# A two-block model in fp32r parts on one core: MLP bias rows in parts, softmax scaling moved to ScalarE, attention heads begun inside projections, and turns of the identity ahead of five waits

## The reference

```
def first_block(x, c, positions, ...):
    for i in range(2):
        shift, scale, gate = modulation(silu(c), mod_mix_w[i], mod_mix_b[i])
        h = x * (1.0 + scale) + shift
        y = mla_mixer(h, ...) if i == 0 else s5_mixer(h, ...)
        x = layer_norm(ALPHA * x + (1.0 + gate) * y, ...)
        shift, scale, gate = modulation(silu(c), mod_ffn_w[i], mod_ffn_b[i])
        a = relu((x * (1.0 + scale) + shift) @ w1 + b1)
        x = layer_norm(ALPHA * x + (1.0 + gate) * ((a * a) @ w2 + b2), ...)
    return x

def second_block(x, ...):
    for l in range(2):
        x = macaron_ffn(x, ...)             # x + 0.5 * rms_norm(swiglu(rms_norm(x)))
        xn = rms_norm(x)
        if l == 0: m = recurrent_block(xn)  # RG-LRU, ends in (h * gelu(y)) @ w_out + b_out
        else:      m = moba_attention(xn @ w_q, k, v, rel_bias) @ w_o
        x = x + rms_norm(m)
        x = macaron_ffn(x, ...)
        if l == 0: k, v = shared_kv(x)
    return x
```

## Time and profile before

| | |
|---|---|
| median of 3 runs | 1750.84 us (1749.12 to 1753.19) |
| profiled execution | 1750.2 us |
| its span, first to last instruction | 1748.6 us |
| mean granted TensorE clock | 0.969 of full |
| PE busy | 1646.2 us (94%) |
| DVE, ACT, POOL busy | 1147.3, 839.1, 153.8 us |

### The profile page before, as it was taken

How to read it: one execution, slowest core, us unless ns; L and a number is a source line. 1 busy time by engine, 2 the same in 40 slices (tenths; PEclk the granted TensorE clock), 3 DMA queues, 4 the chain that set the end, 5 groups by cost and what they waited for, 6 DMA issues and landing times.

```text
span 1748.6 us, 20517 instructions
## 1 busy us (share of the span) xinstructions
PE 1646.2 (94%) x8221; PEld 1327.7 (76%) x8221; DVE 1147.3 (66%) x1354; ACT 839.1 (48%) x1134; POOL 153.8 (9%) x293
## 2 busy tenths in 40 slices
PE   7778999988988999999999999999999999799998
PEld 3656787875677788878888868888788888578887
DVE  4699778888969665575546876544754546665554
ACT  3553465544234555544335875334634435553433
POOL 4510100026600100000000000000000000000000
PEclk9878999999999999999999989999999999899999
DMA  9838588752036566445654554555555554245551
GB/s 305 310 126 308 185 302 332 288 214 100 1 142 220 193 227 238 161 168 192 225 184 141 199 189 171 192 192 169 207 178 183 186 188 167 96 144 193 193 191 74
DMA packets 145096, 335.45 MB, mean 192 GB/s; under 512 B 18213, under 2 KB 34061, under 8 KB 143850
## 3 DMA queue, kind: packets, MB, share of 16 engines
q1 hardware_dynamic: 134310, 293.65, 48.8%
q0 software_dynamic: 9696, 37.29, 5.6%
q10 hardware_dynamic: 996, 3.20, 0.5%
HBM read 328.86 MB, written 6.83 MB: 192 GB/s over the span
## 4 chain that ended last, share of the span: by engine, by line
PE 71%; DVE 16%; ACT 5%; issue 4%; POOL 2%; DMA 1%; SPq 1%; DVEq 0%; ACTq 0%; POOLq 0%
PE ps L670 22%; PE ps L672 22%; PE ps L671 22%; DVE wlo L1794 3%; PE ps L755 2%; ACT whi L1253 1%; DMA operands<-in_mod_mix_w 1%; PE ps L749 1%; DVE work L2247 1%; DVE xlo L1799 1%; PE ps L762 1%; DVE B L1927 1%; POOL mod L2509 1%; DVE B L1926 1%; DVE small L1859 1%
## 5 line engine op out<-in xcount | busy, mean ns | idle before, releaser
L1794 DVE TENSOR_TENSOR wlo<-raw,whi 128x2048 fp32r<-128x2048 f32 (+2 forms) x247 | 559.8, 2283 | 253.5 <-ACT whi L1253 252.2
L1253 ACT ACTIVATE whi<-raw 128x2048 fp32r<-128x2048 f32 (+2 forms) x247 | 466.9, 1908 | 233.9 <-PE ps L672 170.5
L670 PE MATMUL ps<-whi,xhi 128*128 128x512 f32 (+2 forms) x1244 | 477.5, 384 | 18.9 <-DVE xlo L1799 17.3
L672 PE MATMUL ps<-whi,xlo 128*128 128x512 f32 (+2 forms) x1244 | 471.8, 379 | 0.0
L671 PE MATMUL ps<-wlo,xhi 128*128 128x512 f32 (+2 forms) x1244 | 471.7, 379 | 0.0
L670 PE MATMUL ps<-whi,hhi 128*128 128x512 f32 x736 | 294.6, 400 | 6.2 <-DVE hlo L1799 5.2
L671 PE MATMUL ps<-wlo,hhi 128*128 128x512 f32 x736 | 289.0, 393 | 0.0
L672 PE MATMUL ps<-whi,hlo 128*128 128x512 f32 x736 | 288.8, 392 | 0.0
L670 PEld LDWEIGHTS ps<-whi,xhi 128*128 128x128 f32 x1244 | 235.5, 189 | 64.6 <-DVE xlo L1799 21.0
L672 PEld LDWEIGHTS ps<-whi,xlo 128*128 128x128 f32 x1244 | 235.5, 189 | 44.2
L671 PEld LDWEIGHTS ps<-wlo,xhi 128*128 128x128 f32 x1244 | 235.8, 190 | 41.7
(11 more groups left out here) (371 smaller groups left out, 1599.8 us busy)
## 6 DMA issues: line engine op xcount, KB each, us to landing
raw<-in_mlp_w SPq DMA_DIRECT2D x64, 1024.0 KB, 5.6
raw<-in_ffn_w_gate SPq DMA_DIRECT2D x44, 1024.0 KB, 5.1
raw<-in_ffn_w_up SPq DMA_DIRECT2D x44, 1024.0 KB, 5.2
raw<-in_ffn_w_down SPq DMA_DIRECT2D x44, 1024.0 KB, 4.9
mod<-in_mod_ffn_w POOLq DMA_DIRECT2D x16, 1024.0 KB, 6.9
mod<-in_mod_mix_w POOLq DMA_DIRECT2D x12, 1024.0 KB, 7.4
operands<-in_mod_mix_w SPq DMA_DIRECT2D x8, 1024.0 KB, 8.5
raw<-in_lru_w_in SPq DMA_DIRECT2D x8, 1024.0 KB, 5.2
```

Source lines behind the costliest of these rows:

```text
L670: pe.matmul(o, lh, rh, start=start, stop=False)
L672: return pe.matmul(o, ll, rh, start=False, stop=stop)
L1253: act.activation(whi[:, c % SPL, 0:n], raw[:, c % RAW, 0:n], ACT.Copy).then_inc(hi_done, 1)
L1794: dve.tensor_tensor(wlo[:, c % RAW, 0:n], raw[:, c % RAW, 0:n], whi[:, c % SPL, 0:n].bitcast(F32), ALU.subtract).then_inc(lo_done, 1)
```

## The change

Six edits, in one diff.

- **Bias rows of the MLPs.** `open_acc` is gone from `mlp`. Instead `down(..., biased=name)` of the first hidden slice issues, for each bank, two one-row fp32r matmuls ahead of the first product, after the waits for `brow_lo_ok` and `hid_ok`. The row's high part is an ACT copy of 1x1024 (and, for `mlp0`, a copy of the ones), between `hi(c+4)` and `hi(c+5)`. Its rest is a DVE operation of 1x1024 between `lo(c+4)` and `lo(c+5)`.
- **Turns of the identity.** `keep_busy(bank, n)` turns the identity `n` times into a free bank: 14 in `turn(name, 1)` of `mlp0`, `s5` and `ffn10`, 28 in `mla` ahead of `zn_ok`, 32 in `s5` ahead of `g_ok`.
- **First attention.** The rotary queries of heads 0 to 3 are turned before the second half's rotary projection, and `attention` begins after `q_ok` 2 and `qt_ok` 1; the other turns and waits stand in `beside_attention`. ACT's `hi(5)` stands between its two copies of the rotary queries.
- **Softmax scaling.** In both attentions DVE only takes the reciprocal, into `recips`; ACT scales the probabilities of head `i-1` by two copies after the exponentials of head `i`.
- **Second attention.** The scores of heads 0 and 1 stand between the projections of tiles 0 and 1 of the second slice, those of head 2 after tile 1, ahead of the turns. ACT's copies and `hi(c+5)`, `hi(c+6)` are interleaved; DVE's `lo(c+6)` moves into step 0.
- **LRU.** `open_acc("lru")`, with its wait `lg_ok`, stands ahead of `turned(3)`.

```diff
@@ down
+                        if biased and k == 0:
+                            half = slice(512 * n, 512 * (n + 1))
+                            pe.matmul(ps[:, 2 * tt + n, :], ones_r[0:1, :], brow_hi[:, half], start=True, stop=False)
+                            last = pe.matmul(ps[:, 2 * tt + n, :], ones_r[0:1, :], brow_lo[biased][:, half], start=False, stop=False)
+                            if tt and n:
+                                last.then_inc(acc_open, 1)
+            def keep_busy(bank, n):
+
+                for _ in range(n):
+                    pe.transpose(ps[:, bank, 0:P], ident[:, :], ident[:, :])
@@ turn
+                if tt and name in ("mlp0", "s5", "ffn10"):
+                    keep_busy(x_bank(1, 0), 14)
@@ mlp on PE
-                    if i == 0:
-                        open_acc(name)
                     for tt in range(T):
+                        if i == 0:
+                            acc_ready(name, tt)
+                            pe.wait_ge(brow_lo_ok, MLPS.index(name) + 1)
                         pe.wait_ge(hid_ok, HID0[name] + 2 * i + tt + 1)
-                        down(mlp_down(name, i, 0), 4 * (i % 2), tt)
+                        down(mlp_down(name, i, 0), 4 * (i % 2), tt, biased=name if i == 0 else None)
@@ mla on PE
+                keep_busy(0, 28)
                 for tt in range(T):
                     pe.wait_ge(zn_ok, tt + 1)
...
+                    if g:
+                        turn_rotary(0)
...
-                pe.wait_ge(q_ok, 4)
-                pe.wait_ge(qt_ok, 2)
+                pe.wait_ge(q_ok, 2)
+                pe.wait_ge(qt_ok, 1)
                 attention(0, qT, kT, V, True)
@@ s5 on PE
+                keep_busy(6, 32)
                 pe.wait_ge(g_ok, 2)
@@ lru on PE
-                turned(3)
                 pe.wait_ge(lg_ok, KT)
                 open_acc("lru")
+                turned(3)
                 pe.wait_ge(hg_lo, 1)
@@ mlp on ACT
                 hi(c + 4)
+                if l == 0:
+                    act.activation(ones_r[:, :], ones[0:1, :], ACT.Copy)
+                act.wait_ge(brow_in, 16 * (l + 1))
+                act.activation(brow_hi[:, :], brow[name], ACT.Copy).then_inc(brow_hi_ok, 1)
                 hi(c + 5)
@@ attention on ACT
+                    if 1 <= i <= HEADS:
+                        s = (i - 1) % 3
+                        act.wait_ge(rc_ok, HEADS * n + i)
+                        for tt, (lo, up) in enumerate(((0, P), (P, 3 * P))):
+                            last = act.activation(sms[:, s, lo:up], sms[:, s, lo:up], ACT.Copy, scale=recips[:, 2 * s + tt:2 * s + tt + 1])
+                        last.then_inc(p_ok, 1)
@@ mlp on DVE
                     lo(c + j)
+                    if j == 4:
+                        dve.wait_ge(brow_hi_ok, MLPS.index(name) + 1)
+                        rest(brow_lo[name][:, :], brow[name], brow_hi[:, :]).then_inc(brow_lo_ok, 1)
@@ attention on DVE
-                        do(dve.reciprocal(newton[:, 0:2], atts[:, 2 * s:2 * s + 2]))
-                        dve.tensor_scalar(sms[:, s, 0:P], sms[:, s, 0:P], newton[:, 0:1], None, ALU.mult)
-                        dve.tensor_scalar(sms[:, s, P:3 * P], sms[:, s, P:3 * P], newton[:, 1:2], None, ALU.mult).then_inc(p_ok, 1)
-                        dve.wait_ge(p_ok, e + 1)
+                        dve.reciprocal(recips[:, 2 * s:2 * s + 2], atts[:, 2 * s:2 * s + 2]).then_inc(rc_ok, 1)
```

More of the change, by code:

```diff
@@ L708, in project_narrow, with down @@
                 last.then_inc(pe_pass, 1)
-            def down(c, tile, tt, first=False, final=False, src=(hhi, hlo)):
+            def down(c, tile, tt, first=False, final=False, src=(hhi, hlo), biased=None):
                 chunk_ready(c)
@@ L965, in mla, with turn_rotary @@
                 spread_third(1, (6, 7))
+            def turn_rotary(g):
+                pe.wait_ge(qp_ok, g + 1)
+                for r in range(2):
+                    for tt in range(T):
+                        last = pe.transpose(ps[:, 4 * g + 3, r * L + tt * P:r * L + (tt + 1) * P], qp_tok[:, g, tt, r * P:(r + 1) * P], ident[:, :])
+                last.then_inc(qt_ps, 1)
             def z_pass(c, tt):
@@ L997, in beside_attention @@
             def beside_attention(i):
+                if i == 0:
+                    turn_rotary(1)
                 if i == 1:
+                    pe.wait_ge(q_ok, 4)
+                    pe.wait_ge(qt_ok, 2)
                     same_step()
@@ L1020, in beside_attention, with scores, attention @@
                     spread_third(0, (6, 7))
-            def attention(n, q, k, v, rotary):
+            def scores(n, i, q, k, rotary):
+                h, e = i, HEADS * n + i
+                if i >= 3:
+                    pe.wait_ge(sm_ok, e - 2)
+                for lo, hi, tt, keys in ((0, P, 0, P), (P, 3 * P, 1, L)):
+                    last = pe.matmul(ps[:, h % 3, lo:hi], q[:, h, tt * P:(tt + 1) * P], k[:, h, 0:keys], start=True, stop=not rotary)
+                    if rotary:
+                        a = 64 * (h % 2)
+                        last = pe.matmul(ps[:, h % 3, lo:hi], qpT[a:a + 64, h // 2, tt * P:(tt + 1) * P], kpT[a:a + 64, 0:keys],
+                                         start=False, stop=True)
+                last.then_inc(s_ps, 1)
+            def attention(n, q, k, v, rotary, scored=0):
                 sms, pts = (sm, sm2)[n], (pt, pt2)[n]
                 for i in range(HEADS + 3):
[L1026 to L1030, removed]
-                            last = pe.matmul(ps[:, h % 3, lo:hi], q[:, h, tt * P:(tt + 1) * P], k[:, h, 0:keys], start=True, stop=not rotary)
-                            if rotary:
-                                a = 64 * (h % 2)
-                                last = pe.matmul(ps[:, h % 3, lo:hi], qpT[a:a + 64, h // 2, tt * P:(tt + 1) * P], kpT[a:a + 64, 0:keys],
-                                                 start=False, stop=True)
-                        last.then_inc(s_ps, 1)
+                    if scored <= i < HEADS:
+                        if n and i == 4:
+                            pe.wait_ge(feat_ok, FEAT0["att"] + 4)
+                        scores(n, i, q, k, rotary)
                     if 2 <= i < HEADS + 2:
@@ L1185, in att @@
                     token_turn("att", 0, tt)
-                for tt in range(T):
-                    project("att", c + 3, slice_bank(1, tt), tt, 1)
+                project("att", c + 3, slice_bank(1, 0), 0, 1)
+                acc_ready("att", 1)
+                pe.wait_ge(feat_ok, FEAT0["att"] + 2)
+                scores(1, 0, qT2, kT2, False)
+                scores(1, 1, qT2, kT2, False)
+                project("att", c + 3, slice_bank(1, 1), 1, 1)
+                scores(1, 2, qT2, kT2, False)
                 for tt in range(T):
                     token_turn("att", 1, tt)
-                acc_ready("att", 1)
-                pe.wait_ge(feat_ok, FEAT0["att"] + 4)
-                attention(1, qT2, kT2, V2, False)
+                attention(1, qT2, kT2, V2, False, scored=3)
                 for tt in range(T):
@@ L1506, in mla @@
                     act.activation(qpT[:, 2 * g:2 * g + 2, :].rearrange("p r l -> p (r l)"), ps[:, 4 * g + 3, :], ACT.Copy).then_inc(qt_ok, 1)
[L1507 removed]
+                    if g == 0:
+                        hi(5)
                 attention(0)
@@ L1716, in att @@
                 hi(c + 4)
-                hi(c + 5)
                 for tt in range(T):
                     feature_copy("att", 0, tt, qT2)
-                for tt in range(T):
-                    token_copy("att", 1, tt, c + 3, x_scale("ffn11", tt))
+                hi(c + 5)
+                token_copy("att", 1, 0, c + 3, x_scale("ffn11", 0))
                 hi(c + 6)
+                token_copy("att", 1, 1, c + 3, x_scale("ffn11", 1))
                 for tt in range(T):
@@ L2187, in attention @@
                         piece(6)
+                    if n and i == 0:
+                        lo(FIRST["att"] + 6)
             def s5():
@@ L2361, in att @@
                 c = FIRST["att"]
-                for j in range(3, 7):
+                for j in range(3, 6):
                     lo(c + j)
```

19 lines of the change are left out of this document (11 added, 8 removed).

## The result

The changed kernel takes 1768.61 us in the median (1767.83 to 1769.27, 4 runs), the kernel before 1751.30 (1749.12 to 1753.19): a ratio of 1.0102, 95% interval 1.0087 to 1.0117. It is slower, as forecast, but by 17.3 us (medians) where 9.5 was forecast, and outside the range. The profiled execution has a span of 1767.3 us, 18.7 more than before, at the same mean clock of 0.969.

What follows compares the result with a forecast made beforehand. PE was taken to bound the kernel (71% of the chain, busy 94% of the span). The terms summed to +10.25 us, taken as +9.5 on 1750.2, giving 1759.7; range 1750 to 1765.5.

Steps and rivals of the forecast that it cites:

- MLP bias rows, +6.0: Both MLPs at `hid_ok`: DVE's rest 1.2 us plus eight exposed rows 1.8, +3.0 each; bounds +1.9 to +9.6 for both.
- eight one-row matmuls of 512 columns: Behind each MLP's wait for `hid_ok`: priced from three products at 0.227 us each, 1.8 in all.
- The clock falls behind this wait before as after: At the MLPs' `hid_ok`: PE's first product takes 0.79 us against 0.39 later; no added cost in the sum.
- Turns in the turns of tile 1, +3.3: 14 identity turns each: `mlp0` +1.15, `s5` +1.6, `ffn10` +0.55; bounds +2.5 to +4.5.
- None of the three places shows a fall of the clock that 14 turns could prevent: `mlp0`, `s5` and `ffn10`, turns of tile 1: no clock gain was credited to the 14 turns.
- `zn_ok` and `g_ok`, 0 and −1.45: 28 turns in `mla` hidden in a wait, 0; 32 in `s5` return half of 2.9 us at half clock, −1.45.
- First attention, −1.2: Earlier DVE start and scalings moved to ACT give up to −4.8; POOL's chain and moved PE turns up to +2.
- POOL's chain does not move: First attention: PE's turns at step 1 wait for ACT's copies of `wide_row`, and these for POOL, holding the second step.
- Second attention, +2.65: Scalings in ACT's ring, 0.71 us a step, about +3.75; start 1.1 earlier; bounds +0.5 to +4.5.
- LRU, +0.95: Before the second down projection: rows made earlier gain at most 1.35, a clock restart costs about 2.3; bounds −1.35 to +2.
- The full clock through the attentions: Rival, chance 0.17: denser start keeps PE at full clock, first attention returns up to 11.5 us; faster, 1746 with 14.5.
- The rival in which DVE and ACT make room: Rival, chance 0.20: bias rows' rest hides, first attention gives −4.8, LRU −1.35; +2 in sum, 1752, no change.

Runs made afterwards that it cites:

- the kept parts: Kernel before plus late first attention with scalings on ACT, second attention's early scores with scalings on DVE, and 32 turns ahead of `g_ok`: 1746.69 us.
- rows ahead: Changed kernel with the eight fp32r one-row MLP bias matmuls issued in one run ahead of the wait for `hid_ok`: 1757.46 us.
- rows first: Changed kernel with all eight one-row matmuls in one run behind the wait for `hid_ok`, ahead of the first product: 1764.17 us.

## Why the prediction was right or wrong

**MLP bias rows, +6.0: wrong in size, 11.8 by the traces and 11.9 by the experiment.** The mechanism was right: the rows were hidden ahead of `hid_ok` and are exposed behind it. The step that failed is "eight one-row matmuls of 512 columns", priced from three dense products at "0.227 each", "1.8 us in all": a pair among products takes 0.77 to 0.87, eight rows 3.1 to 3.4. The same part said "The clock falls behind this wait before as after", and the sum had nothing for it. It does fall in both, but PE then works 7.6 and 7.8 us at half rate instead of 5.8 and 2.8, which is 0.9 and 2.5 us. The term's upper bound, +9.6, was too low too. DVE's rest was 1.1 us in the trace, as forecast.
The Trainium skill (TensorE: Matmul & The Clock Gate, Part 1) has activity release the throttle. Here PE is busy 16.0 of 17.1 us at half clock with rows of one partition among its products, so a PE that is busy in the timeline can still be at 1.2 GHz; why isn't shown by these runs.

**Turns in the turns of tile 1, +3.3: right for the PE time, wrong as a price.** They take 1.53 us each, and cost 1.13, 1.53 and 0.55 where they stand, 3.2 in all; but the kernel without them is 8.0 us slower, and the kept parts with them only 0.9 slower. Where no pairs stand among the products, the kernels without the turns are 3.2 us (rows ahead) and 2.9 us (rows first) slower; so some 5 of the 8 us are the pairs' stretch at half clock, 17.1 instead of 10.2. That half the turns do as well as all speaks for the moment at which PE comes back, and against their number. The other 3 us lie in stretches at half clock at other places. The step "None of the three places shows a fall of the clock that 14 turns could prevent" fits the trace before, and failed in `ffn10` for other timings: of the seven kernels here without turns there, five have a stretch at half clock (3.4 or 6.8 us) right behind the turns of tile 1, and of the eleven with them (14, or 7 in one) none. In `mlp0` and `s5` it stays open whether the loss is owed to the turns or to chance, as does what picks 10.2 or 17.1. The moment by itself doesn't: PE comes back in `mlp0` at 203.99 in the kernel without turns and at 203.91 in the one with the scalings on DVE, and the stretches are 17.1 and 10.2 us.

**`zn_ok` and `g_ok`, 0 and −1.45: right in kind.** Ahead of `g_ok` the turns kept the clock at 1.00 through the wait; −1.8 in the trace, and 3.5 by the experiment, with 2.3 in place. The 28 turns ahead of `zn_ok` were not undone by themselves. In the trace the delay grows by 0.15 us there, and PE is at half clock from 62.6 to 66.0 all the same, as it was at this place before (58.2 to 65.0).

**First attention, −1.2: wrong in sign, +2.25.** The failed step is "POOL's chain does not move" with "the POOL chain stretched by 1.2". I saw that an earlier DVE meets more of POOL, but counted only the row of one lengthened scaling. POOL's own instructions are stretched as well: its chain went from 13.4 to 16.7 us, beginning 1.0 later. PE waits for it at step 2 and not at step 1, where the prediction has it, so it is the scores of head 3 that it holds back. Undoing the start gives 3.0 us back, holding DVE's additions 3.8 (3.4 and 3.3 in place, by the traces).
The Trainium skill (SBUF — State Buffer, on the shared port pair) has DVE and GpSimd lock each other out. The trace agrees that both lose: 1.06 us became 2.04 for the same POOL instruction, 1.28 became 2.05 for DVE's addition.

**Second attention, +2.65: right.** A step of 3.99 us (4.08 forecast), begun 1.2 sooner (1.1), +2.0 in all. Without the copies on ACT the end comes 4.2 us sooner in place (3.75 forecast), and 2.4 by the medians of the kept parts.

**LRU, +0.95: right.** +1.15 with the wait of 5.12 us and the stretch at half clock behind it that were forecast; 2.6 by the experiment, 1.5 of it in place. The 2.3 for the restart had no row of its own; PE works 5.15 us at half clock there, which is 2.6.

**The sum.** The bias rows are 5.8 us over their term, the first attention 3.45, and 0.85 came in ahead of all edits; the other terms together are 1.85 under theirs. The step from the sum, 10.25, down to 9.5 was a guess about the clock without a row, and the clock went the other way.

**Rivals.** The full clock through the attentions did not come: the first attention still has 20.5 us at half (89.9 to 110.4), though PE is busy in only 9.0 of them. The rival in which DVE and ACT make room needed a POOL chain that holds nothing up; PE waited 11.46 us for it.

## What to carry to other kernels

Work that stands ahead of a wait is free up to the wait's length, and behind it costs its whole time; price it there from a row of the same shape among its new neighbours, not from a denser one. A full PE is not a PE at full clock: compare the stretches at half clock of both kernels before believing any difference of a few us, since stretches in instructions that no edit touched changed by 7 us (`mlp1`, 10.2 or 17.1) when PE came back 0.3 or 2.3 us later. And before starting an engine earlier, look at what then runs beside it: DVE began 4.4 us sooner, and POOL's chain, which the path waits for, became 3.3 us longer.

## What the runs showed of the hardware

A one-row fp32r matmul of 512 columns takes 0.23 us from start to start behind its like, and 0.33 in pairs between 128-row products, at full clock. With such rows behind the wait for `hid_ok`, in pairs or in one run, PE stayed at 1.2 GHz for 7.1 to 16 us of work, against 2.8 to 6.3 without. The effects of edits do not add: undoing each alone of those that the kept parts undo gives 11.9 + 3.0 + 2.6 − 8.0 + 0.9 = 10.4 us (the 28 turns, which weren't undone alone, cost 0.15 by the trace, and the 0.9 has both attentions' scalings in it), while undoing them together gives 21.9.
